# A hybrid decoder step on one core: gates finished in the projection, page sums moved into it, and the tail's first weights split during retention

## The reference

```python
z = u @ w_in                       # u = rms_norm(h); splits: fq fk fv fl rq rk rv g
logf = log_sigmoid(fl + b_f)       # per row and head, for forgetting attention
fo = fox attention(fq, fk, fv, cumulative sums of logf; past pages with their own sums)
ro, S = retention over chunks of 128 rows, with rotary rq and rk; the samples from state_ret
ro = (ro - mean) * rsqrt(var + eps) * gn_w          # per head
mix = (concat([fo, ro]) * silu(g)) @ w_out
h = h + mix;  h = h + sigmoid(h @ gate_w) * rms_norm(p @ proj)
```

## Time and profile before

| | us |
|---|---|
| median of three runs | 4061.73 |
| the profiled execution | 4048.7 |
| its span, first to last instruction | 4047.1 |
| PE busy | 3530.1 (87%) |
| DVE busy | 1653.4 (41%) |
| ACT busy | 1374.3 (34%) |
| POOL busy | 414.5 (10%) |

### The profile page before, as it was taken

The page is one execution under the profiler, slowest core; times in us unless marked ns, Lnnn a source line. Parts: engine busy times, 40 slices in busy tenths (PEclk is TensorE's granted clock), DMA queues, the critical chain, the costliest instruction groups (busy, mean ns, idle before and its releaser), DMA issues. The chain is left out here.

```text
span 4047.1 us, 65101 instructions
## 1 busy us (share of the span) xinstructions
PE 3530.1 (87%) x21092; PEld 2650.6 (65%) x21092; DVE 1653.4 (41%) x3094; ACT 1374.3 (34%) x2374; POOL 414.5 (10%) x663
## 2 busy tenths in 40 slices
PE   6999799955799899989999676799987999859998
PEld 5888688843455565555555465688875767548887
DVE  3222311133345444444454266433334666643333
ACT  3111200011233333333333265333335666643222
POOL 0000000001022222222222243000000000000000
PEclk9999899966799999999999887899998999979999
DMA  5233522245577777777776555533324353142221
GB/s 153 105 123 129 159 101 100 94 112 157 158 231 233 219 231 231 227 217 235 233 232 190 171 203 194 178 130 124 118 101 168 112 170 125 54 167 88 88 87 54
DMA packets 381103, 627.45 MB, mean 155 GB/s; under 512 B 124121, under 2 KB 182401, under 8 KB 380802
## 3 DMA queue, kind: packets, MB, share of 16 engines
q1 hardware_dynamic: 339026, 487.55, 37.2%
q0 software_dynamic: 41792, 136.48, 10.8%
HBM read 488.67 MB, written 135.22 MB: 154 GB/s over the span
## 5 line engine op out<-in xcount | busy, mean ns | idle before, releaser
L1549 PEld LDWEIGHTS att_samp_ps_t<-att_ident,att_samp_k_ring 128*128 128x128 f32 x2048 | 238.9, 147 | 281.3 <-issue 231.6
L1549 PE MATMUL att_samp_ps_t<-att_ident,att_samp_k_ring 128*128 128x128 f32 x2048 | 339.5, 291 | 84.3 <-DVE att_samp_kt L1354 44.2
L123 PE MATMUL in_ps_z<-in_w_hi,in_u_hi 128*128 128x512 f32 x952 | 374.0, 393 | 36.6 <-DVE in_w_lo L156 36.6
L1149 POOL DMA_DIRECT2D att_samp_v_ring<-cache_v x512 | 274.8, 537 | 982.1 <-issue 979.7
L125 PE MATMUL in_ps_z<-in_w_hi,in_u_lo 128*128 128x512 f32 x952 | 373.1, 392 | 0.0
L124 PE MATMUL in_ps_z<-in_w_lo,in_u_hi 128*128 128x512 f32 x952 | 372.9, 392 | 0.0
L1239 ACT COPY att_samp_kt<-att_samp_ps_t 128x512 f32<-128x512 f32 x256 | 149.8, 585 | 501.8 <-PE att_samp_ps_t L1549 500.4
L1354 DVE COPY att_samp_kt<-att_samp_ps_t 128x512 f32<-128x512 f32 x256 | 176.3, 689 | 292.3 <-PE att_samp_ps_t L1549 287.2
L1503 PE MATMUL att_fox_ps_o<-att_fox_prob,att_fox_v_one 128*65 128x512 f32 (+3 forms) x640 | 286.9, 532 | 3.8 <-ACT att_fox_prob L1208 3.8
L1303 DVE TENSOR_REDUCE att_fox_part_max<-att_fox_ps_n 128x1 f32<-128x512 f32 (+2 forms) x320 | 195.1, 610 | 128.4 <-PE att_fox_ps_n L1470 112.3
L1208 ACT ACTIVATE att_fox_prob<-att_fox_ps_k 128x512 f32<-128x512 f32 (+1 forms) x320 | 169.9, 536 | 187.4 <-DVE att_fox_ps_k L1322 110.0
(11 more groups left out here) (366 smaller groups left out, 6859.7 us busy)
## 6 DMA issues: line engine op xcount, KB each, us to landing
att_samp_v_ring<-cache_v POOLq DMA_DIRECT2D x512, 256.0 KB, 3.8
att_samp_k_ring<-cache_k SPq DMA_DIRECT2D x512, 256.0 KB, 3.5
tail_a_hi<-a_hi SPq DMA_DIRECT2D x34, 512.0 KB, 5.9
tail_a_lo<-a_lo SPq DMA_DIRECT2D x34, 512.0 KB, 6.0
in_w_stage<-w_in_even SPq DMA_DIRECT2D x64, 256.0 KB, 6.2
lru_u_hi<-u_hi SPq DMA_DIRECT2D x8, 2048.0 KB, 8.0
lru_u_lo<-u_lo SPq DMA_DIRECT2D x8, 2048.0 KB, 13.1
in_x<-x SPq DMA_DIRECT2D x17, 512.0 KB, 3.8
```

Of the source, the lines that this page charges most:

```text
L123: pe.matmul(out, act_hi, w_hi, start=start, stop=False)
L1149: pool.dma_start(v_ring[:, p, g, :], row(io["cache_v"], page)).then_inc(vp_in[y], 16)
L1549: last = pe.transpose(ps_t[:, a * PAGE:(a + 1) * PAGE], k_ring[:, n % 2, p, a * P:(a + 1) * P], ident[:, :])
```

## The change

Three parts, and what goes with them.

1. In half 1 of `in_proj`, ACT reads each gate group twice (times 0.5, and tanh of half), DVE joins the two to silu, and for g1 POOL multiplies by the norm weight. The stage leaves finished gates in g0 and g1. `retention` loses tanh, silu and the weighing.
2. `forget_gates` is gone as a stage, and the page sums are gone from the sample retention: `GatesAside` does both during tiles 10 to 16 of half 1, one slice of work after each tile's own (`PEEL` = 7 tiles are written out for that). Its tables are loaded behind the first 8 weight pieces. The sample retention now interleaves state updates with outputs.
3. The tail's first 20 pieces (`ple_proj`, `w_out_even`) get tiles that live over both stages (`TailWeights`) and are loaded and split during `retention`, one per step, through seven buffers: ACT the high part, POOL the low part. The tail keeps 16 pieces, through four buffers.

In `retention` the order and the buffers also change: five q/k/v buffers for three, three for `q_dec`, two each for the masked scores, for `a_hi` and `a_lo` and their stores.

```diff
 def in_proj(nc, io, half):                                 # half 1
+            if not first: sp.dma_start(gn, ret_gn_w broadcast)        # first of all
             fetch(0, 0)
             weights.load(sp, 0, KC)
+            if not first: side.load(sp)      # identity upper ones scan_mask, 4x index, later, keep
             fetch(1, 1)
 # ACT, per tile
+    act.activation(half_z[:, g - 2, :], ps_z[:, g, :], ACT.Copy, scale=0.5)
+    act.activation(tanh_z[:, g - 2, :], ps_z[:, g, :], ACT.Tanh, scale=0.5)
+    side.on_scalar(act, t)
 # DVE, per tile
-    dve.tensor_scalar(z[:, g, :], ps_z[:, g, :], 0.5, None, ALU.mult)
+    dve.scalar_tensor_tensor(z[:, 2, :] or silu_z, tanh_z, 1.0, half_z, ALU.add, ALU.mult)
+    side.on_vector(dve, t)   # n = t - 10: low part r=n-2, difference r=n-1, reorder and scan r=n
 # POOL, per tile
+    pool.tensor_tensor(z[:, 3, :], silu_z[:, :], gn[:, :], ALU.mult)
+    side.gather(pool, t)
 # SP, per tile: stores of z, then side.store(sp, t) (new_logf, neg_cum, 4 x rel), then fetch(t + 2)
 # PE, after group 3 of a tile: side.on_tensor(pe, t)  (2 sums, 1 transpose, 4 x page totals)
-def forget_gates(nc, io): ...
 def sample_retention(nc, io):                              # was past_gates_and_...
 # PE: the update of head h now stands behind the outputs of head h; the transposes back come last
 def retention(nc, io, held):
 # DVE step(t)
     reduce; variance
+    if prompt(t): add_update(t)
     reciprocal; normed
     gated[:, t % 2, W:] = normed * gate[:, t % 2, W:]      # was silu_gn
-    decay_q(t + 2); gate_silu(t + 1); add_update(t + 1); cut(t); decay_scores(t + 2)
+    cut(t - 1); decay_scores(t + 2); decay_q(t + 3)
 # ACT step(t)
-    sqrt; place(t + 2); tanh_gate(t + 1); keep_o(t + 1); a_hi(t); square(t + 1)
+    sqrt; place(t + 3); weights.make_high(piece t); keep_o(t + 1); a_hi(t); square(t + 1)
 # POOL, per step
-    decay_k(t + 1); scale_state(t + 1); weigh_gates(t + 1)            # two multiplies
+    scale_state(t + 1); decay_k(t + 2); gate_fox(t + 2); weights.make_low(piece t + 1)
 # PE step(t)
-    turn_qk(t + 2); attend(t + 1); turn_gated(t); turn_rows(t + 1); add_to_state(t + 1); score(t + 2)
+    score(t + 2); attend(t + 1); turn_gated(t); turn_rows(t + 1); add_to_state(t + 1); turn_qk(t + 4)
 # SP step(t)
+    weights.load(piece t + 6)
     wait u_done(t); fetch_qkv(t + 5)                       # was t + 3
     wait fox_gated(t), gated_rows(t); fetch_gate(t + 2)
     wait a_low(t); store a_hi, a_lo
 def tail(nc, io, layer, held=None):
 # layer 0: no loads and splits of the first 20 pieces; gate pieces 0 to 7 are split after square_e(0),
 # 8 to 15 after cut_h1(0), through the four halves of u_hi and u_lo
```

More of the change, by code:

```diff
@@ L248, in _ @@
             weights.load(sp, 0, KC)
+            if not first:
+                side.load(sp)
             fetch(1, 1)
@@ L657, in _ @@
                           start=True, stop=True).then_inc(updated, 1)
+            pe.wait_ge(o_kept, 1)
+            for h in range(H):
+                last = pe.transpose(ps_b[0:ROWS, h * HD:(h + 1) * HD], o_t[:, h, :], ident[0:HD, 0:HD])
+            last.then_inc(back, 1)
         @block.scalar
         def _(act):
-            def cut_high(r):
-                act.wait_ge(behind, r + 1)
-                if r >= 2:
-                    act.wait_ge(rel_stored[r % 2], 16 * 2 * (P // NP) * (r // 2))
-                act.copy(cut[:, r % 2, 0], rel[:, r % 2]).then_inc(high, 1)
-            cut_high(0)
-            cut_high(1)
             for n in range(2):
@@ L1627, in _, with retention @@
             each_tile(pe, step, H, peel=2)
-def retention(nc, io):
+def retention(nc, io, held):
     with ExitStack() as ctx:
@@ L2047, in tail @@
         u_lo = ph.sb("u_lo", [P, D], F32R) if first else None
-        weights = SplitWeights(ph, pieces, 2 if first else 6,
-                               [u[:, g * G:(g + 1) * G].bitcast(F32) for u in (u_hi, u_lo) for g in range(2)] if first else ())
+        if kept:
+            us = [u[:, g * G:(g + 1) * G].bitcast(F32) for u in (u_hi, u_lo) for g in range(2)]
+            ahead = len(held.pieces)
+            gate_weights = SplitWeights(ph, more, 0, us)
+        else:
+            ahead = 0
+            weights = SplitWeights(ph, held.pieces + more, 6)
+            gate_weights = weights
+        gate_base = GATE - len(gate_weights.pieces)
         stat = ph.sb("stat", [P, 8])
@@ L2833, in trunk @@
         in_proj(nc, io, 1)
-        forget_gates(nc, io)
-        past_gates_and_sample_retention(nc, io)
+        sample_retention(nc, io)
         attention(nc, io)
-        retention(nc, io)
-        tail(nc, io, 0)
+        with ExitStack() as kept:
+            held = TailWeights(Phase(nc, kept, "held"), io, 0)
+            retention(nc, io, held)
+            tail(nc, io, 0, held)
         lru(nc, io)
```

619 lines of the change are left out of this document (352 added, 267 removed).

## The result

The changed kernel takes 3972.8 us, the kernel before 4060.9 beside it: a ratio of 0.978, with an interval of 0.9761 to 0.9799. Of the four executions behind 3972.8 one took 6243.3 us at a granted clock of 0.672 (the others 3967.8 to 3975.3 at 0.941 to 0.943), and of the ten of before_peel7 one 4706.7 at 0.725; the ratios leave these two out, and without them the medians are 3970.3 and 4049.1, which the table of experiments has. The profiled execution took 3970.3 us, its span 3968.7.

What follows compares the result with a forecast made beforehand. PE was busy 87% of the span, so only stretches where PE waits could give much. 4.5 + 2.5 + 2.5 - 11.0 - 9.7 - 40.5 - 12.0 = -63.7: 3985.0 us profiled, 3998 beside the median; range 3975 to 4024.

Steps and rivals of the forecast that it cites:

- Half 1, +9.5: Projection's half 1: +4.5 us at the start for added table loads, +2.5 in steady tiles, +2.5 at the end.
- Forget stage: The separate forget-gate stage disappears, its work lying inside half 1's tiles: -11.0 us.
- Sample retention, -9.7: Sample retention falls from 70.8 to 61.1 us, with first PE work at 19.6; bounds -3 and -18.
- I take -1: Sample retention's start: the 2.1 MB gather no longer shares queues with the state, -1 us, between 0 and -8.
- the rival of 2.4 GHz there: Sample retention at 2.4 GHz: the 29.3 us of outputs and updates becomes 14.7, the kernel 3983 us; 4%.
- Retention, -40.5: Retention: 15 steps fall from 11.83 to 9.0 us (bounds 8.1 and 10.5), plus 2 us before the first `normed`.
- the ring, cycle 2: Retention: two gate buffers, so load, POOL's queue and DVE's update take 17.6 us per two steps, 8.8 a step.
- The first rival: Retention: gate ring decides, landing grows from 4.8 to 8 us; step 10.4, retention -19.5, kernel 4019 us; 18%.
- The +2 before the first `normed`: Retention's start: more PE products stand ahead of the first centring, +2 us, between 0 and 4.
- The slower rival: Retention with PE at 1.2 GHz throughout: PE's 15 us a step bind, +50 there, kernel 4088 us; 5%.
- Tail, -12: Tail's start: gate's second group 33 us after PE's first work, not 46.1; -13, -12 kept, bounds -18 and -5.
- The offset, +13: Whole kernel: the profiled execution lay 13.0 us below the median 4061.73, so 13.0 was added back to the sum.

Runs made afterwards that it cites:

- before_peel7: The kernel before with seven instead of three tiles of the projection's half 1 written out behind its loop: 4049.1 us, ratio 0.9987.
- late_tables: The changed kernel with the loads for the projection's gates issued behind all 32 weight pieces instead of ahead of 24: 3966.3 us, ratio 0.977.
- best: The changed kernel with POOL's forget-attention product a step later, tables loaded behind the weight pieces, variance folded into ACT's square root: 3945.9 us, ratio 0.9731.
- issues_back: The changed kernel with SP again issuing the sample retention's six former first loads, into memory nothing reads, without the gather: 3972.9 us, ratio 0.980.
- update_mid: The changed kernel with state update, low part and score mask ahead of the sum of squares again, behind q's decay: 4008.2 us, ratio 0.988.

## Why the prediction missed

*Half 1, +9.5.* +11.3. From the stage's start to its first store it was +5.1 (49.4 against 44.3) for the +4.5 forecast; late_tables and best show that the tables ahead of the pieces are 4.9 and 3.9 of it. Tiles and end were as forecast within 2 us.

*Forget stage.* Right.

*Sample retention, -9.7: the term "I take -1" for the gather failed.* The bounds were 0 and -8, and I chose by the argument that SP's 11.4 us were many short runs. The hold fell by 7.0, and putting the gather back brought more than that again. PE's first work came 13.7 us in instead of the forecast 19.6: of the 9.9 us gained on the kernel before, issues_back shows 3.9 for the six issues (-3 forecast), which leaves 6.0 to the gather. The rest held: 5.4 us from PE's first work to the first output, 29.2 us (868.14 to 897.3) of interleaved outputs and updates against 29.3, then 5.7 for 6.8, at a clock of 0.50 as forecast, so the rival of 2.4 GHz there is out.

*Retention, -40.5.* The sum is nearly right (-38.7) by luck in part, its mechanism half. I took 9.0 as the chain with a slow attend. In fact the attend is mostly fast (in 12 of 15 steps 1.05 or 1.13 us for its first part), the chain 8.27 (7.59 forecast; I didn't foresee the 0.76 by which the variance is held, about the difference), and the mean of 9.28 comes from the ring, cycle 2, in some of the steps: PE's granted clock was 0.94 between 2308 and 2428. The first rival ("the gate ring decides", 10.4) is what the long steps look like, by the path that the prediction named as its sign (state decay on POOL late behind the gate multiply): the load that lets POOL start at 2380.70 took 6.6 us from its issue, for the 4.8 of the earlier trace rows. I had costed the piece's issue on SP at 0.45 us; it mostly took 0.73 to 0.82, and 2.04 in the long step. The +2 before the first `normed` was wrong in sign: it came 29.5 us in, 34.0 before. The end, put at nothing, grew: from the last `normed` of the prompt to the tail's first load 22.8 us, 18.8 before. So the 15 steps gave -38.3 where -42.5 was forecast, and the start's -4.5 and the end's +4.0 nearly cancel; no run took these two apart. The slower rival, PE at 1.2 GHz throughout, did not come; update_mid shows a milder form of it from 2352 on, 0.86.

*Tail, -12: the second group's term failed.* PE's first work, its gate groups, and the landing of the gate pieces by the DMA issues (count, KB, median us):
```profile
2477.18 0.66 PE L2397 MATMUL tail_ps_g<-tail_ident,tail_p 128*128 128x128 f32 x2 [15.11 <-DMA tail_p<-p]
2498.23 0.50 PE L123 MATMUL tail_ps_g<-tail_wg_hi,tail_h_hi 128*128 128x512 f32 x1 [0.96 <-DVE tail_h_lo L2338]
2505.78 0.49 PE L123 MATMUL tail_ps_g<-tail_wg_hi,tail_h_hi 128*128 128x512 f32 x1 [1.82 <-DVE tail_wg_lo L157]
```
```profile
tail_u_hi<-ple_gate_w SPq DMA_DIRECT2D x8, 256.0 KB, 3.4
tail_u_lo<-ple_gate_w SPq DMA_DIRECT2D x8, 256.0 KB, 3.6
```
From PE's first work at 2477.18 the groups start 21.1 and 28.6 us later, for 23 and 33 forecast, so the second follows 7.6 us behind the first instead of 10. It waited 1.82 us; the forecast meant some 4.3 (10 less the 5.7 that the first group takes). The 4.4 us of landing was the wrong row: 16 of its 20 loads belong to the other layer's tail, and the loads here took 3.4 and 3.6. That is about 0.9 of the 2.4 us by which the second group came closer; where the rest of it and the 2 us before the first group come from, no run took apart. PE's first work came 1.1 us sooner (6.5 us in), which was put at nothing, and the 1 us kept back for a PE at the low clock was not needed.

*The attention, 0.* -4.4. The sum put this stage at nothing without giving a reason; its cause stays open.

*The offset, +13.* The first profiled execution lay 13 us under its median, the second one of that kernel 2.1 above the median of its neighbours (4055.3), and that of the changed kernel 2.5 under 3972.8 (it is itself the 3970.3). Adding a whole offset of one execution was a step of the sum that failed, by 10.5 (13.0 against 3970.3).

Together: 1.8 - 7.1 + 1.8 - 6.7 - 4.4, with -0.1 elsewhere, is -14.7 on the profiled execution, and -10.5 by the offset: 3998 - 25.2 = 3972.8. All large misses went the same way. Only the gather's was a choice near the small end of its bounds (-1 of 0 to -8); the tail's -12 stood in the middle of -5 to -18 and came out at -18.7, and the attention and the offset had no bounds at all.

## What to carry to other kernels

When a wait moves to another engine, list what stands behind it in that engine's queue: moving one multiply behind the state decay took 12.6 us out of the retention (5.5 against the shortest of the unchanged ones) and made the staging, worth nothing before, worth 15.8. An order on the engine that closes a loop can cost twice: here the old one cost 2.3 us a step at a clock of 1.00 (10.56 against 8.27) and 1.4 more at 0.86. And where two bounds are far apart, as for the gather, a small step that decides between them (which bytes share the queue with the long load) is better than taking the near end.

## What was not expected of the hardware

A DVE instruction on 128 x 8 values takes 0.17 us alone and 0.93 beside a POOL product, another form of it 0.92 there; the inverse beside POOL takes 0.20. Loads that move 2.1 MB by a gather made a neighbouring issue on SP hold 13.6 us instead of 4.4. Peeling four tiles of a loop took two pauses of 3.6 and 3.8 us out of a later stage whose code was the same, left two others there, and didn't make its profiled time shorter. A loop with the same pause of 2.62 us in every step ran three steps at a granted clock of 1.00 and the rest at 0.82 to 0.86.
